# Columns of four experts selected at once, in a hybrid encoder layer with a mixture of experts

## The reference, cut to what matters

```
f = hierarchical MoE(h):                      # h is (512, 1024)
    group   = argmax of 4 group logits        # top 1
    experts = top 2 of the 8 in the group     # 32 experts in all
    y[token] += weight * (silu(h[token] @ w_gate[e]) * (h[token] @ w_up[e])) @ w_down[e]
x = LN(alpha * x + gate2 * f)
```

## Time and profile before

| | us |
|---|---|
| median of three executions (961.78, 965.32, 965.1) | 965.1 |
| the profiled execution | 966.24 |
| its span, first to last instruction | 964.6 |
| TensorE busy | 914.6 |
| VectorE busy | 382.2 |
| ScalarE busy | 244.7 |

### The profile page before, as it was taken

One profiled execution on the slowest core, in us unless ns is written; L12 is line 12 of the kernel. 1 busy time (PEld: TensorE's weight loads), 2 busy tenths in 40 slices (PEclk: granted clock), 3 DMA queues, 4 the chain that ended last, 5 costly groups with the idle time before them and its releaser, 6 DMA issues.

```text
span 964.6 us, 11484 instructions
## 1 busy us (share of the span) xinstructions
PE 914.6 (95%) x4257; PEld 539.9 (56%) x4257; DVE 382.2 (40%) x666; ACT 244.7 (25%) x357; POOL 113.2 (12%) x142
## 2 busy tenths in 40 slices
PE   3799999999999999999999999999998999999994
PEld 2477676888888888787344344434443443444331
DVE  4522443465354246798532223213222221232135
ACT  2422333441334325445411011101100110111024
POOL 2120367000001000000000000000000000000031
PEclk9799999999999999999999999999999999999997
DMA  9975654356464622909999999999999699999964
GB/s 370 343 227 216 240 201 179 123 194 241 175 250 143 196 87 100 292 1 392 380 385 426 426 426 427 428 426 427 426 429 426 284 429 427 427 428 427 422 269 139
DMA packets 47509, 295.51 MB, mean 306 GB/s; under 512 B 5046, under 2 KB 7190, under 8 KB 32082
## 3 DMA queue, kind: packets, MB, share of 16 engines
q1 hardware_dynamic: 37216, 263.99, 67.8%
q0 software_dynamic: 9616, 29.02, 9.1%
q10 hardware_dynamic: 610, 1.66, 0.5%
HBM read 275.81 MB, written 23.09 MB: 310 GB/s over the span
## 4 chain that ended last, share of the span: by engine, by line
PE 86%; DVE 3%; ACT 3%; issue 3%; SPq 2%; DMA 1%; DVEq 0%; ACTq 0%
PE bank L609 83%; PE bank L885 2%; SPq L382 2%; ACT x_rows L1115 2%; DMA modraw<-in_w_mod 1%; PE bank L666 0%; DVE wo_lo L1685 0%; DVE y_second L2092 0%; DVE y_second L2105 0%; ACT w_hi L1115 0%; PE bank L903 0%; DVE bank L2100 0%; DVE g_a L1702 0%; DVE res L1745 0%; DVE z_row L1754 0%
## 5 line engine op out<-in xcount | busy, mean ns | idle before, releaser
L609 PE MATMUL bank<-up_w,x_t 128*64 128x512 f32 x512 | 225.0, 592 | 0.0
L609 PE MATMUL bank<-gate_w,x_t 128*64 128x512 f32 x512 | 225.0, 592 | 0.0
L609 PEld LDWEIGHTS bank<-gate_w,x_t 128*64 128x64 f32 x512 | 70.1, 137 | 143.1 <-issue 143.1
L609 PE MATMUL bank<-h_hi,w_hi 128*128 128x512 f32 x320 | 126.0, 394 | 1.6 <-ACT h_hi L1149 1.6
L609 PE MATMUL bank<-h_hi,w_lo 128*128 128x512 f32 x320 | 125.8, 393 | 0.0
L609 PE MATMUL bank<-down_w,hid_t 128*64 128x512 f32 x512 | 118.8, 606 | 6.4 <-issue 6.0
L609 PE MATMUL bank<-h_lo,w_hi 128*128 128x512 f32 x320 | 124.6, 397 | 0.0
L1349 ACT ACTIVATE sg_hid<-bank 64x512 f32<-64x512 f32 x33 | 19.6, 593 | 350.7 <-PE bank L609 350.7
L1962 DVE TENSOR_TENSOR sg_hid<-bank,sg_hid 64x512 f32<-64x512 f32 x32 | 22.2, 695 | 201.6 <-ACT sg_hid L1349 201.6
L1520 DVE TENSOR_TENSOR w_lo<-raw,w_hi 128x1024 fp32r<-128x1024 f32 x56 | 68.5, 1225 | 79.0 <-ACT w_hi L1115 78.9
L581 POOL DMA_INDIRECT round_y<-yout,store_row x31 | 31.3, 1010 | 487.7 <-DVE yout L1980 461.3
(11 more groups left out here) (319 smaller groups left out, 1107.1 us busy)
## 6 DMA issues: line engine op xcount, KB each, us to landing
down_w<-in_w_exp_down SPq DMA_DIRECT2D x32, 2048.0 KB, 18.3
gate_w<-in_w_exp_gate SPq DMA_DIRECT2D x30, 2048.0 KB, 17.9
up_w<-in_w_exp_up SPq DMA_DIRECT2D x30, 2048.0 KB, 22.4
modraw<-in_w_mod SPq DMA_DIRECT2D x24, 1024.0 KB, 6.7
raw<-in_w_in SPq DMA_DIRECT2D x9, 2048.0 KB, 9.8
round_y<-zrow POOLq DMA_DIRECT2D x6, 2048.0 KB, 7.6
raw<-in_w_branch_b SPq DMA_DIRECT2D x2, 2048.0 KB, 9.5
raw<-in_w_branch_a SPq DMA_DIRECT2D x2, 2048.0 KB, 10.8
```

Of the source, the lines that this page charges most:

```text
L609: return pe.matmul(out, lhsT, rhs, start=start, stop=stop, skip_group_check=True)
```

## The change

`sel` for two experts gives way to `sel_group` for four, compared once every four experts. The selection changes its operands' roles: h's pieces are now the weights (128 tokens by 128 features of one chunk), and the 4 x 64 slots of four experts move through. The result is already columns: features on partitions, 256 slots. So there are no rows to copy and no transposes for experts 4 to 31. A bank holds two chunks of features (a "pair of chunks"); eight chunks for four experts are four such pairs, and each expert's turn does one: 16 matmuls of 256 columns, 12 ahead of the hidden transposes and 4 behind them. The first group (experts 4 to 7) is selected in the turns of experts 2 and 3, two pairs each; those of experts 28 to 31 have none. ScalarE copies the pair (`pair_columns`), VectorE no longer copies columns for these experts. Two layouts of the columns share one place in SBUF and alternate between groups. Experts 0 and 1 keep the old way, and 2 and 3 get their columns by it. Some tiles move to other places.

In a further round the pair comes first, then the further selection; the further gate and up come ahead of the main down product instead of behind it.

```diff
+        def columns_of(e, kc):
+            if e // 4 % 2 == 0:
+                return x_by_expert[:, e % 4, kc, :]
+            return x_by_pair[:, kc // 2, e % 4, kc % 2, :]
+        def pairs_selected(e):
+            return {2: (0, 1), 3: (2, 3)}.get(e, (e,) if 4 <= e < NEXP - 4 else ())
...
+            def chunk_selected(kc, tiles):
+                for i in tiles:
+                    for piece in (h2_hi, h2_lo):
+                        x = mm(B[2][:, 256 * (kc % 2):256 * (kc % 2) + 256], piece[i][:, kc, :], sel_group[:, i, :, :].rearrange("p a s -> p (a s)"),
+                               start=(i == 0 and piece is h2_hi), stop=(i == TILES - 1 and piece is h2_lo))
+                return x
+            def pair_begun(n):
+                pe.wait_ge(m_sem["sl"], 4 + n // 4)
+                pe.wait_ge(m_sem["xt"], 5 + n)
+                chunk_selected(2 * (n % 4), range(TILES))
+                chunk_selected(2 * (n % 4) + 1, range(2))
+            def pair_ended(n):
+                chunk_selected(2 * (n % 4) + 1, range(2, TILES)).then_inc(m_sem["xs"], 1)
...
-                    pe.wait_ge(m_sem["xt"], 3 if e == 1 else e - a + 3)
-                    gate_up(x_t[:, 2 * a:2 * a + 2, :, :], s, B[0], m_sem, halves=(e_gu[s], loaded) if last else None)
+                    pe.wait_ge(m_sem["xt"], 3 if e == 1 else 5 + 4 * (e // 4))
+                    gate_up(partial(columns_of, e), s, B[0], m_sem, halves=(e_gu[s], loaded) if last else None)
...
-                select_next(e)
-                residual_ahead(e)
-                main_transposes(e)
-                next_columns(e)
-                main_down(e)
+                else:
+                    pairs = pairs_selected(e)
+                    for n in pairs[0:1]:
+                        pair_begun(n)
+                    residual_ahead(e)
+                    main_transposes(e)
+                    for n in pairs[0:1]:
+                        pair_ended(n)
+                    main_down(e)
+                    for n in pairs[1:]:
+                        pair_begun(n)
+                        pair_ended(n)
...
             def with_further(e):
                 more, first = turns_of(e)
+                for n in pairs_selected(e):
+                    pair_begun(n)
+                    pair_ended(n)
                 further_selected(first)
                 main_transposes(e)
                 further_columns(first)
+                further_gate_up(e, first)
                 main_down(e)
-                further_gate_up(e, first)
-                select_next(e)
                 further_transposes(first)
-                next_columns(e)
                 further_down(e, first)
...
+            def pair_columns(n):
+                act.wait_ge(m_sem["xs"], 6 + n)
+                p = n % 4
+                out = x_by_pair[:, p, :, :, :] if n // 4 % 2 == 0 else x_by_expert[:, :, 2 * p:2 * p + 2, :]
+                copy(out, B[2][:, :].rearrange("p (c a s) -> p a c s", c=2, a=4)).then_inc(m_sem["xt"], 1)
...
-                if e < NEXP - 2:
-                    rows_in(e + 3 if e < 2 else e + 4, B[2])
+                if e < 2:
+                    rows_in(e + 3, B[2])
                 hid_columns(m_sem, B[3], hid_t, e)
+                for n in pairs_selected(e):
+                    pair_columns(n)
...
+            def chosen_group(first):
+                dve.wait_ge(m_sem["xs"], 1 + first)
+                dve.tensor_tensor(sel_group[:, :, :, :],
...
-                out_rows(e)
                 further_gate(e, first)
                 further_hidden(first)
-                next_chunks(e)
+                out_rows(e)
+                next_group(e)
                 further_out(first)
...
                     gate_rows(e)
-                    next_chunks(e)
                     out_rows(e)
+                    next_group(e)
```

More of the change, by code:

```diff
@@ L3 @@
 from contextlib import ExitStack
+from functools import partial
 D = 1024
@@ L892, in gate_up @@
                         pe.wait_ge(*halves)
-                    mm(bank[0:CAP, :], xt[:, kc // 4, kc % 4, :], gate_w[s][:, kc, :], start=(n == 0), stop=(n == KC - 1))
-                    x = mm(bank[CAP:128, :], xt[:, kc // 4, kc % 4, :], up_w[s][:, kc, :], start=(n == 0), stop=(n == KC - 1))
+                    mm(bank[0:CAP, :], xt(kc), gate_w[s][:, kc, :], start=(n == 0), stop=(n == KC - 1))
+                    x = mm(bank[CAP:128, :], xt(kc), up_w[s][:, kc, :], start=(n == 0), stop=(n == KC - 1))
                     if half_done is not None and n == KC // 2 - 1:
@@ L1340, in _ @@
                 act.wait_ge(m_sem["xtr"], h + 1)
-                copy(x_t[:, 0:2, 2 * h:2 * h + 2, :],
+                copy(x_by_expert[:, 0, :, :].rearrange("p (c k) s -> p c k s", c=2)[:, :, 2 * h:2 * h + 2, :],
                      B[4 - 2 * h][:, 256 * h:256 * h + 256].rearrange("p (k c s) -> p c k s", k=2, c=2)).then_inc(m_sem["xt"], 1)
@@ L1939, in further_round @@
                 further_out(turns)
[L1941 to L1953 removed]
+            def chosen_group(first):
+                dve.wait_ge(m_sem["xs"], 1 + first)
+                dve.tensor_tensor(sel_group[:, :, :, :],
+                                  slots[:, :].rearrange("p (i a s) -> p i a s", i=1, a=1).broadcast_to([128, TILES, 4, CAP]),
+                                  slot_of[:, first:first + 4, :].rearrange("p a (i s) -> p i a s", s=1).broadcast_to([128, TILES, 4, CAP]),
+                                  ALU.is_equal).then_inc(m_sem["sl"], 1)
             def sides(e):
@@ L1968, in gate_rows, with next_group @@
                 gate_of_slots(yout[s], dve_g, 2 * (e // 3 + 1) + 2 * e, side[:, 0, s:s + 1], side[:, 1, s:s + 1])
-            def next_chunks(e):
-                if e < NEXP - 2 and e % 2 == 0:
-                    first_chunks(e + 4)
-                elif e < NEXP - 2:
-                    last_chunks(e + 4, B[2])
-                    next_pair(e + 3)
+            def next_group(e):
+                if e % 4 == 3 and e + 5 < NEXP:
+                    chosen_group(e + 5)
             def out_rows(e):
@@ L2016, in expert @@
                     gate_rows(e)
-                    first_chunks(4)
-                    last_chunks(5, B[4])
-                    next_pair(4)
+                    for half, bank in enumerate((B[2], B[4])):
+                        dve.wait_ge(m_sem["xtr"], 4 + half)
+                        columns_in(x_by_expert[:, 2:4, 4 * half:4 * half + 4, :], bank).then_inc(m_sem["xt"], 1)
+                    chosen_group(4)
                     out_rows(e)
```

48 lines of the change are left out of this document (20 added, 28 removed).

## The result

The changed kernel takes 968.11 us in the median (20 executions, 964.59 to 972.58), the kernel before 964.49 us (20, 960.28 to 967.87). The ratio is 1.0047, 95% interval 1.0034 to 1.0060: slower by 0.5%, where 0.5% faster was forecast. The profiled execution took 971.62 us, its span is 969.9 us, against 966.24 and 964.6: 5.3 us more of span. The ratios and mean clocks of this document leave out one disturbed execution, of e4 (1553.15 us).

A forecast was written before the change was run, and what follows sets the result against it. Weights and TensorE both near their limit: weights bind before expert 19, TensorE from 765 us. +0.5 - 3.8 - 1.4 = -4.7, less 0.3 for the end, -4.4 us: 960.7 us against the 965.1 median, range 956.8 to 965.4.

The forecast's parts named there:

- The plain expert: Experts 4 to 27: 256-column matmuls at 0.121 us, hidden transposes not waiting, 0.47 us gained an expert, period 13.35 us.
- Rivals 1 and 4: First: cheaper columns, hidden rows bind, 958.4 us, 17%; fourth: 256-column matmuls wait for weight loads, 969 or 975 us, 8%.
- Experts 20 to 27: Plain experts behind expert 19's further round: 8 x 0.47 = 3.8 us gained, reaching the end.
- Experts 28 and 29: No selection stands there now; TensorE waits for hidden rows and their copy: 0.72 us gained each, 1.4 together.
- rival 2: Longer waits slow the clock; a fall behind expert 18's down product ends expert 19 1.7 us later: 962.4 us, 15%.
- The lead of the weights: Expert 31's last gate part lands at 914, wanted at 922.1, so no more than about 8 us of gain can pass.
- Rival 3: Weights bind behind expert 19 too, so only the 0.65 us of earlier issue count: 964.5 us, 15%.
- Experts 2 and 3: Two pairs of chunks each make TensorE 3.3 us later together; cost at the end nothing, 3.3 us without that cover.
- Expert 19: Its further round: gate part 22 issued at 762.7 instead of 763.36, further down product 0.5 us later (-1 to +2.5).
- The end: Experts 30 and 31 stay and the gathers stand nearer the last weights: 0.3 us taken off the gain.

The follow-up runs named there:

- e4: Kernel before without the selections, row copies and column transposes in the turns of experts 28 and 29: 963.96 us, ratio 0.9992.
- e1: Changed kernel plus 16 unused 256-column matmuls in each of the turns of experts 28 and 29: 965.12 us, ratio 0.9998 to the kernel before.
- e10: Changed kernel with unused matmuls in experts 28 and 29, plus 4 more in each of experts 20 to 27: 965.50 us, ratio 1.0010 to the kernel before.
- e3: Changed kernel with 2 matmuls instead of 16 for the second pair of chunks in experts 2 and 3: 968.74 us, ratio 1.0037 to the kernel before.
- e7: Changed kernel with unused matmuls in experts 28 and 29 and expert 19's pair behind the further gate and up: 963.20 us, ratio 0.9992 to the kernel before.
- e5: Changed kernel loading only one eighth of expert 24's up part: 964.41 us, ratio 0.9995 to the kernel before.
- e2: Changed kernel with the main down product again ahead of the further gate and up in a further round: 970.17 us, ratio 1.0051 to the kernel before.
- e6: Changed kernel with expert 19's pair behind the further gate and up instead of ahead of the further selection: 965.52 us, ratio 0.9999 to the kernel before.
- e9: Changed kernel, unused matmuls in experts 28 and 29; further round: main down, further gate and up, then pair: 963.76 us, ratio 1.0000 to the kernel before.

## Why the prediction was wrong, step by step

**The plain expert** was right: 0.12 us a matmul, transposes not waiting, 13.37 us forecast as 13.35. The forecast's 0.121 us was an estimate of mine and no run of before shows it: rows 4 have 0.23 us for 512 columns, rows 6 give 0.111 for a load; the changed kernel's 256-column matmuls are spaced 0.12 (862.41 to 863.01, five spacings). Rivals 1 and 4 are out with it. **Experts 20 to 27** were right: 3.8 us were won by expert 28's silu. The waits for down parts from 652 to 732 us (1.41, 1.69, 1.66 and 1.80 us) were as forecast too, about 1.5.

**Experts 28 and 29** are the step that failed: "0.72 us each, 1.4 together" as a gain. The profile has 3.9 us lost, and e1 gives back 4.7 by the ratios. I had counted the bare waits as a shorter path, with weights that are there and a clock that stays up. Under these two conditions the figure was right: in e4 an expert takes 13.2 us there (13.1 forecast). In the changed kernel neither held. I had weighed what waits do to the clock for expert 18 alone (rival 2), not for the two places where the change itself opened waits: the bare 1.5 and 0.5 us met the next error, and with 0.99 us more of waiting the 48 matmuls behind them took 13.20 us instead of 10.5.

**The lead of the weights** was read at the wrong place: "no more than about 8 us can", from the gate part and the down part of expert 31. The scarcest lead is at down part 28. In the kernel before it is issued at 867.4 and lands 20.6 us later, at 888.0, and is wanted at 891.2: 3.2 us. Behind it the queue gives down part 29 next, issued at 881.2, landed 11.7 us later, at 892.9, and wanted at 904.9; the lead there is 12.0 us. In the changed kernel down part 28 lands at 868.4 + 23.5 = 891.9, 3.9 us later, and is wanted at 891.0. The time to landing of the two:

```profile
down_w<-in_w_exp_down SPq DMA_DIRECT2D x1, 2048.0 KB, 20.6
...
down_w<-in_w_exp_down SPq DMA_DIRECT2D x1, 2048.0 KB, 23.5
```

A gain of 3.8 us in experts 20 to 27 could not pass there in full: with the filler TensorE stands 1.60 us (e1), with the gain taken back not at all (e10). Rival 3 was right in kind. And the 16.7 us of rows 8 are those of the first half of the last up part; in e4's profile the second halves of gate and up take 19.2 and 21.5 us.

**Experts 2 and 3** "cost nothing": the thin stretch came (382 GB/s for 408), and weights up to expert 18 were later for it, in these profiles by 1 to 2 us; e3 shows the cause. For TensorE the two cost 4.4 us by expert 4's silu, not 3.3: 0.8 us more is a wait of expert 4's gate product for ScalarE's copy of the last pair, a term left out. For the end it cost nothing that e3 could measure.

**Expert 19**: the clock fell behind the 1.80 us wait at expert 18's down part, as rival 2 had it, 1.7 us in expert 19's products (12.2 for 10.5). In e7 and e10 it did so behind 1.85 and 1.86 us, in e1 and e5 there was no such wait (0.07 and 0.11) and no fall; but it also fell behind 1.12 us in e4 and did not behind 1.35 in the kernel before. For the round itself I had the parts right (bare copy, bare wait, half clock under the pair: gate part 22 18.5 us after the first matmul, by my figures 762.7 - 744.25 = 18.45). In e1 and e5, where the round begins sooner, gate part 22 is issued at 762.90 and 762.17, as forecast (762.7), and expert 20's silu comes at 777.9 and 777.1, before at 777.1 (0.5 later forecast):

```profile
762.90 0.33 SPq L411 DMA_DIRECT2D gate_w<-in_w_exp_gate  x1
```

So this step is not shown to be wrong; the 4.4 us at expert 20 are in the main the falls of the clock in one execution. That silu 19 to silu 20 is 36.6 us here and 36.2 before, 0.4 later for 0.5, is luck in part: in e4, e1 and e5 it is 33.3, 35.5 and 35.6.

**The end**: silu 31 to the end of the span is 36.4 us instead of 35.6. The chain passes through the gather. I had allowed 0.3 us for the end, and it took 0.8; in the other profiles with the new columns it takes 35.7 to 36.6 us, so part of that may be scatter.

Sum of the profile: 4.4 at expert 20 (for 0.5), minus 3.8 (for minus 3.8), plus 3.9 (for minus 1.4), plus 0.8 (for 0.3): 5.3 us. The medians have 3.6. What holds over the executions is the gain of 3.7 or 3.8 us in experts 20 to 27 and a loss from expert 28 to the end, 2.3 to 5.4 us in the profiles of the changed kernel, e2 and e3 (79.1 to 82.2 us for 76.8), where a gain of 1.1 was forecast.

Open: whether late weights or late TensorE is worth more behind expert 20 (e10's interval), how much the change costs up to expert 20 (the profiles scatter by up to 4 us there), and why the clock fell in e5, e6 and e9 and not in e4 with as much idle time.

## What to carry to other kernels

Where a buffered stream of loads and an engine run at nearly the same rate, look for the transfer with the least lead over the whole stretch, not for the lead at the end; here a gain of 3.8 us met a lead of 3.2 us at down part 28, and TensorE waited there for 0.99 us, with the filler for 1.60. When work is moved away from a place where it covered a wait, price the bare wait with the clock in it: here two experts lost 3.9 us where 1.4 were to be won, and 1.9 us of unused matmuls in each brought the time of the kernel before back (ratio 0.9998, e1). The pair did better behind the product that frees the weight buffer than ahead of it (4.6 us less by the ratios, e6). And before a profile is read as the account of a median, compare its time and its mean clock with those of the other executions: here 1.7 us of the 5.3 are not in the medians.

## What the runs showed of the hardware

The granted clock fell to 0.5 for 3.4 or 6.8 us at a time, in experts 28 and 29 (3.4 and 6.8 us behind expert 28's waits in e5 and the changed kernel) behind idle stretches of TensorE of at most 2.1 us each (in e3 0.39 us for the copy and then 1.68 for the weights). How busy TensorE was just before does not tell a fall from none in these rows: over the 5 us from expert 28's silu on it was busy 3.03 us in e4, where the clock stayed at 1.00, and 3.01 in e5 and 2.94 in e6, where it fell; and it fell behind a wait of 1.58 us (e9) and not behind one of 1.60 (e1). Executions of one kernel differ in it: 0.971 to 0.984 in the mean for the changed kernel. A 256-column float32r matmul with fresh 128-column weights is spaced 0.12 us (862.41 to 863.01 in the changed kernel), half of a 512-column one (0.23, 609.28 to 610.43 in the kernel before), so the load adds nothing that shows. At half clock the same matmul is spaced 0.21 us (748.39 to 751.39 in the changed kernel, 14 spacings). With TensorE's issues 2 us later (514.17 for 512.19) and a down part still landing until 518.4, the transfers moved 388 GB/s from 514 to 520 us instead of 431, and 325 in e1.
